# The fifth choice behind the fourth naming, other slots at which gather buffers join a ring, and the first query panel loaded into an area of its own

## The reference

```
u = expert_u[it]
h = jax.nn.gelu(jnp.einsum('td,tkd->tk', xt, u), approximate=False)
v = expert_v[it]
return jnp.einsum('tk,tkd->td', gt * h, v)
```

## Time and profile before

| | us |
|---|---|
| median of 3 runs (1876.32 to 1880.17) | 1878.65 |
| the profiled execution | 1875.81 |
| its span | 1874.0 |
| TensorE busy (matmul) | 1616.2 (86%) |
| VectorE busy | 997.8 (53%) |
| ScalarE busy | 454.4 (24%) |
| GpSimd busy | 314.4 (17%) |
| DMA, mean of the span | 252 GB/s |

### The profile page before, as it was taken

How to read it: one execution, slowest core, us unless ns; L and a number is a source line. 1 busy time by engine, 2 the same in 40 slices (tenths; PEclk the granted TensorE clock), 3 DMA queues, 4 the chain that set the end, 5 groups by cost and what they waited for, 6 DMA issues and landing times.

```text
span 1874.0 us, 19456 instructions
## 1 busy us (share of the span) xinstructions
PE 1616.2 (86%) x7688; PEld 1082.2 (58%) x7688; DVE 997.8 (53%) x1846; ACT 454.4 (24%) x1010; POOL 314.4 (17%) x269
## 2 busy tenths in 40 slices
PE   7999989999897887698938666677999999899998
PEld 6857656764755444245614222226998476479963
DVE  2433334331785775437997766663565414346654
ACT  1142142230333443213323322221000012310001
POOL 0000000000103533323426645520000000000000
PEclk9999989999998989899979988988999999999999
DMA  6444221126886999899999999993544443254443
GB/s 238 173 145 176 85 90 46 58 89 228 330 362 265 395 421 422 348 426 421 419 386 410 422 422 422 421 422 152 209 157 152 158 169 136 78 203 180 155 160 112
DMA packets 55192, 471.32 MB, mean 252 GB/s; under 512 B 6592, under 2 KB 7744, under 8 KB 10432
## 3 DMA queue, kind: packets, MB, share of 16 engines
q0 software_dynamic: 36864, 268.45, 34.6%
q1 hardware_dynamic: 18240, 201.66, 28.5%
HBM read 469.04 MB, written 1.05 MB: 251 GB/s over the span
## 4 chain that ended last, share of the span: by engine, by line
PE 63%; DMA 18%; DVE 10%; ACT 3%; issue 3%; POOL 2%; SPq 0%; DVEq 0%; ACTq 0%; POOLq 0%
PE ps L2381 13%; DMA main<-in_expert_uv,main 11%; PE ps L486 7%; PE ps L442 6%; PE ps L2538 5%; DMA panels<-in_expert_uv,main 5%; PE ps L412 5%; PE ps L1004 4%; PE ps L1242 4%; PE ps L2304 3%; PE ps L2308 3%; PE ps L482 3%; DVE main L938 2%; PE ps L2327 2%; DMA panels<-in_wall 2%
## 5 line engine op out<-in xcount | busy, mean ns | idle before, releaser
L1004 PE MATMUL ps<-main 128*128 128x512 f32 x636 | 320.6, 653 | 79.6 <-ACT main L985 72.8
L920 POOL DMA_INDIRECT main<-in_expert_uv,main x200 | 240.6, 1203 | 353.8 <-PE ps L1004 183.0
L938 DVE SCALAR_TENSOR_TENSOR main<-main 128x1024 f32<-128x1024 f32 x200 | 240.9, 1223 | 101.9 <-DMA main<-in_expert_uv,main 100.7
L1004 PEld LDWEIGHTS ps<-main 128*128 128x128 f32 x636 | 127.8, 210 | 252.5 <-issue 142.1
L1004 PE MATMUL ps<-panels,main 128*128 128x512 f32 x180 | 93.0, 660 | 53.5 <-ACT main L985 46.8
L973 ACT ACTIVATE main<-main 128x2 f32<-128x2 f32 x128 | 25.9, 203 | 399.7 <-DVE main L938 296.6
L442 PE MATMUL ps<-panels,xT 128*128 128x512 f32 x256 | 112.5, 592 | 0.0
L2381 PE MATMUL ps<-main 128*128 128x128 f32 x912 | 104.9, 275 | 0.0
L2381 PEld LDWEIGHTS ps<-main 128*128 128x128 f32 x912 | 103.4, 192 | 0.0
L1004 PEld LDWEIGHTS ps<-panels,main 128*128 128x128 f32 x180 | 36.1, 210 | 105.8 <-issue 70.3
L938 DVE SCALAR_TENSOR_TENSOR panels<-panels,main 128x1024 f32<-128x1024 f32 x56 | 67.5, 1223 | 43.4 <-DMA panels<-in_expert_uv,main 42.9
(11 more groups left out here) (318 smaller groups left out, 2395.0 us busy)
## 6 DMA issues: line engine op xcount, KB each, us to landing
panels<-in_wall SPq DMA_DIRECT2D x88, 2048.0 KB
main<-in_rows SPq DMA_DIRECT2D x14, 512.0 KB, 9.0
main<-in_expert_uv,main POOLq DMA_INDIRECT x200, 20.3
main<-in_sub_keys SPq DMA_DIRECT2D x2, 1024.0 KB, 13.3
mats<-in_mats SPq DMA_DIRECT2D x1, 1088.0 KB, 5.9
x<-in_x SPq DMA_DIRECT2D x2, 512.0 KB, 4.0
main<-in_pool_w SPq DMA_DIRECT2D x1, 1024.0 KB, 33.3
main<-in_rel_bias SPq DMA_DIRECT2D x1, 1024.0 KB, 15.2
```

The lines of the kernel that those rows point to most:

```text
L920: pool.indirect_dma_start(out=self.bufs[self.buf_of[r]], out_offset=None, in_=self.c.dram["expert_uv"], in_offset=bass.IndirectOffsetOnAxi ...
L938: dve.scalar_tensor_tensor(out=u, in0=u, scalar=1.0, in1=self.c.row(m, H2), op0=ALU.mult, op1=ALU.mult, accum_out=self.dots_at[:, m, q:q + ...
L1004: mm = pe.matmul(self.c.ps[:, b, :], self.diags[self.of_pe(r) % DIAG_RING], v[:, half * HALF:(half + 1) * HALF], start=(q == 1), stop=(q = ...
```

## The change

Four constants change: PANELS_FROM 12 to 15, PARTS_FROM 76 to 84, CHOICE_FREE 40 to 28, and QK_FIRST = 28 is new. In the order, top4, best4 and name4 of tile 0 stand between name3 and the two rows that follow it, and all hgrn1 pieces come after those, with two rows behind each. (So there are 73 rows before hgrn1's state instead of 70, and each later piece up to the cap at 128 comes three rows later.)

By the new spans row 12 gets the buffer of row 4, rows 13 and 14 those of rows 8 and 9, rows 15 to 18 the panel buffers; from 19 to 27 nine buffers go round, rows 28 to 30 get buffers 4 to 6, twelve go round to 59, eight from 60 to 83, and ten from 86. The row at CHOICE_FREE in tile 1 is now 156 instead of 168.

The ring of panels no longer holds qk's first panel: PLAN counts three for qk and WALL_AT skips one. SyncE loads the first into the 4096 floats from area 28 on, right behind the down panel that it issues at q = 3 of `stream`, with a semaphore of its own. The products with it are written out in `attention_tensor`, and use the two banks of the other parity; `keep_qk` reads them there. The loop of `stream` for down0 is no longer rolled, as its panels aren't consecutive in the wall.

```diff
-PLAN += WEIGHTS[[x for x, _ in WEIGHTS].index("ff0"):]
+PLAN += [(x, n - (x == "qk")) for x, n in WEIGHTS[[x for x, _ in WEIGHTS].index("ff0"):]]
...
-WALL_AT = [IN_WALL[x.split(".")[0]] + q for x, n in PLAN for q in range(n)]
+WALL_AT = [IN_WALL[x.split(".")[0]] + q + (x == "qk") for x, n in PLAN for q in range(n)]
...
-    def stream(self, sp, name, less=0):
+    def stream(self, sp, name, less=0, ahead=None):
...
             sp.wait_ge(self.panel_done.sem, first + q - 1)
             sp.dma_start(self.panels[:, slot, :], wall[at[q]]).then_inc(self.panel_loaded[slot].sem, 16)
+            if ahead == q:
+                sp.dma_start(self.area(D * QK_FIRST, PANEL), wall[IN_WALL["qk"]]).then_inc(self.first_qk_loaded.sem, 16)
...
-PANELS_FROM = 12
+PANELS_FROM = 15
 PANELS_UNTIL = 56
-PARTS_FROM = 76
-CHOICE_FREE = 40
+PARTS_FROM = 84
+CHOICE_FREE = 28
...
     part("beside1", 5)
     part("tile0", "name3")
     part("read1", 5)
+    part("tile0", "top4", "best4", "name4")
     rows(2)
     labels = ["k_t"] + [f"{x}{l}" for l in range(LEVELS) for x in ("span", "both", "a", "pick")]
-    for x in ("top4", "best4", "name4"):
-        part("hgrn1", labels.pop(0))
-        rows(1)
-        part("tile0", x)
-        part("hgrn1", labels.pop(0))
-        rows(2)
     for x in labels + ["ends"]:
         part("hgrn1", x)
         rows(2)
...
+        self.first_qk, self.first_banks = slot(QK_FIRST, KC, HALF), 2 * (1 - FIRST["qk"] % 2)
...
+        else:
+            pe.wait_ge(c.first_qk_loaded.sem, 16)
         pe.wait_ge(*c.at("xT_read", 2 + m))
-        products_by_tile(c, pe, "qk", (0,), m, True)
-    products_of_both(c, pe, "qk", (1,))
+        for j in range(2):
+            bank = t.first_banks + j
+            if m == 0:
+                pe.wait_ge(c.bank_read[bank].sem, c.bank_uses[bank])
+                c.bank_uses[bank] += 1
+            for half in range(2):
+                for k in range(KC):
+                    at = (2 * j + half) * P
+                    mm = pe.matmul(c.ps[:, bank, half * T + m * P:half * T + (m + 1) * P], t.first_qk[:, k, at:at + P],
+                                   c.xT[:, k, m * P:(m + 1) * P], start=(k == 0), stop=(k == KC - 1))
+            if m == 1:
+                mm.then_inc(c.up("first_qk"), 1)
+    products_of_both(c, pe, "qk", (0,))
...
-    c.stream(sp, "down0")
+    c.stream(sp, "down0", ahead=DOWN_SEVENS - 1)
```

More of the change, by code:

```diff
@@ L260, in __init__ @@
         self.hidden_made = sig("hidden_made")
+        self.first_qk_loaded = sig("first_qk_loaded")
         self.down_combined, self.h_combined = sig("down_combined"), sig("h_combined")
@@ L2689 @@
 ATTENTION_UNITS = ["s0.0", "s1.0", "s1.1", "s0.1", "s1.2", "s1.3", "a0.0", "a1.0", "a1.1", "o0", "o1", "t0", "t1"]
-QK_AT = (0, 2, 1, 3)
+QK_AT, QK_FIRST = (0, 2, 1, 3), 28
 GROUP_UNITS = [[("s0.0",), ("s1.0", "s1.1")], [("s0.1",), ("s1.2", "s1.3")]]
@@ L2762, in attention_tensor @@
     first_two = list(c.bank_uses)
-    products_of_both(c, pe, "qk", (2,), (0,))
+    products_of_both(c, pe, "qk", (1,), (0,))
     turned_back(first_two)
@@ L2766, in attention_tensor @@
     scores(1, 0)
-    products_of_both(c, pe, "qk", (2,), (1,))
+    products_of_both(c, pe, "qk", (1,), (1,))
     scores(1, 1)
-    products_of_both(c, pe, "qk", (3,))
+    products_of_both(c, pe, "qk", (2,))
     all_four = list(c.bank_uses)
@@ L2802, in keep_qk @@
     def keep_qk(q, j):
-        bank, at = wait_product(c, act, "qk", q, j), 4 * QK_AT[q] + 2 * j
+        at = 4 * QK_AT[q] + 2 * j
+        if q == 0:
+            bank = t.first_banks + j
+            act.wait_ge(*c.at("first_qk", 0, j + 1))
+        else:
+            bank = wait_product(c, act, "qk", q - 1, j)
         act.activation(t.qkT[:, at:at + 2, :], c.ps[:, bank, :].rearrange("p (k t) -> p k t", k=2),
```

## The result

The changed kernel takes 1860.85 us (median of 4 runs, 1859.38 to 1861.97) beside 1879.41 us of the kernel before on the same chip (1876.32 to 1884.14): ratio 0.9911, 95% interval 0.9891 to 0.9931, faster by 18.6 us. Measured again later, it took 1865.20 us (6 runs, 1861.74 to 1866.91): ratio 0.9920, interval 0.9900 to 0.9940. The forecast was 1860.7, in a range of 1854 to 1871. The two profiled executions differ by less than the medians: span 1874.0 before, 1860.2 after, 13.8 us.

A forecast was written before the change was run, and what follows sets the result against it. Full DMA engines were taken to bound the gather, so only their idle time could be won: gather 1.0 + 5.6 + 7.4 + 0 = 14.0, plus attention 4.0, 18.0 us; 1857.8, by the median 1860.7, range 1854 to 1871.

The forecast's parts named there:

- Choice 4, VectorE: Tile 0's fourth choice moved ahead of dots 11 and 12: its 16.1 us fill VectorE's 15.30 us gap.
- A: DMA idle at 552 to 573 us, 16.2 us: loses 2.5, gains 1.5, so 1.0 us won.
- B: DMA idle at 600 to 640 us: shrinks from 7.1 to about 1.5, 5.6 us won.
- rival 1: Gap at 600 to 640 us only moves, through later k_t and rows 19 and 20: won 12.4, 1866.3; chance 0.14.
- from slot 28 three more buffers help: Step for the 600 to 640 us gap: three more buffers join from slot 28, before from 40.
- C: DMA idle at 750 to 762 us, at the gate: recurrence buffers from 84 remove it, 7.4 us won.
- D: DMA idle at 970 to 985 us: keeps its 3.1 us, 0 won (bounds 4 lost to 3 won).
- what would show it: Signs listed, among them DMA share above 0.95 from 590 us and gathers ending about 14 us earlier.
- The 8 buffers: Rows 60 to 83 on 8 buffers instead of 12: price of less depth taken as 0.
- rival 4: Slower: 8 buffers don't keep the engines full over slots 60 to 83; 1884.9 at 3.5 us per row; chance 0.04.
- Attention: First query panel loaded aside: 2.5 us less wait and 1.6 us faster products, sum 4.0 us won.
- Rival 2: Tile 1 takes over, TensorE's path from the gate ruling: only 1.3, 3.5 and attention's 4.0 won, 1869.9; chance 0.12.

The follow-up runs named there:

- e4: Changed kernel with the two rows behind tile 0's fourth naming issued right behind the third, ahead of beside1 5 and read1 5; 1862.45 us, ratio 0.9912.
- e10: Changed kernel with CHOICE_FREE back at 40 instead of 28; 1863.33 us, ratio 0.9925.
- e8: Kernel before with the new order of the fourth choice and PARTS_FROM 79, other slots as before, no panel aside; 1876.21 us, ratio 0.9981.
- e7: Kernel before with the three new slot numbers (15, 84, 28), its own order and no panel aside; 1873.19 us, ratio 0.9964.
- e9: Kernel before with one constant changed, PARTS_FROM 84 instead of 76; 1874.94 us, ratio 0.9980.
- e2: Changed kernel with one row instead of two behind each of the first three hgrn1 pieces; 1863.94 us, ratio 0.9923.
- e3: Changed kernel letting rows up to 136 instead of 128 be issued beside tile 1's last two choices; 1859.74 us, ratio 0.9902.
- e12: Changed kernel with the edits of e2, e3 and e4 together; 1858.67 us, ratio 0.9898.

## Why the prediction was right, and where not

**The number.** 1860.7 against 1860.85, but this closeness is luck: the way shrank by 12.6 to 13.3 us where the sum said 18.0, and the first comparison stood some 5 us above that, most likely by chance. The gather, from row 11 to the last row, went from 701.0 to 693.0 us (692.0 in after again), 8.0 to 9.0 us where the sum said 14.0. The direction, the range and most of the steps stand on their own.

**Choice 4, VectorE.** Right. The 15.30 us gap is gone; choice 4 ends at 576.8 (forecast 576.5), dots 11 and 12 at 579.1 (578.8), and k_t runs at 587.47 (about 586) after 8.29 us of idle (about 7).

**A.** Row 12 at 550.38 (forecast 552), row 13 at 571.54 (572.6). Forecast 1.0 won; 0.1 to 1.1 is read. Right in substance: the early row fills what the burst, later against row 11, gives back (row 13 leaves 30.6 us behind row 11, before 30.2). e4 shows what A hangs on, the place of the sums before or behind a 7.3 us product.

**B, 5.6 forecast, 3.2 to 3.6 measured.** The hole at 600 to 640 closed, and a new one of 3.1 to 3.5 us opened ahead of it: row 19 left at 590.22, not 588, and row 20 at 592.09, not 590. That is rival 1 in small:
```profile
590.00:595.00 5.00, 5.00 (x24) 3.12 (x23) 3.27 (x6) 3.92 (x12) 3.56 (x2) 1.00 0.51 177
```
e10 shows that the step "from slot 28 three more buffers help" was wrong; the order alone closes B (e8: B is 0), and what is left of it in after comes with slot 15.

**C, 7.4 forecast.** Right, 7.5 measured, and by the means named: the slot number closes it (e7, e9). Wholly it does so only with the three rows more at the gate, which the working had as well. (Its "about 0.7 us later" should be 7.5 - 6.6 = 0.9; nothing hangs on it.) The gate's end came at 758.0, forecast 756.5; tile 1's first product at 777.28, forecast 777.

**D, the step that failed.** The sum had 0. D grew by 3.9 to 4.7 us. The working had VectorE's choices begin 10.8 us earlier and the add of row 128 come 14.3 us earlier, since three dots fewer stand among them. The choices began 13.2 us earlier (859.58 against 872.77), and 25 dots and not 28 stand among them, as forecast; but the add at 967.38 comes only 9.5 us earlier than that of before at 976.92. VectorE used the head start to wait: 10.1 us for rows that had not landed (the two above and two of 1 us), where before it waited 2.8. The rows came at 2.49 us each whatever VectorE did, and each choice piece now stood behind three later ones. I had taken the step's time for VectorE's work alone, and with it put the price of the later add at nothing. Relative to row 11, row 90 was issued 13.3 us earlier than before, row 142 only 8.3. e2 and e3 show the cause from both sides. In the part on what would show it, two signs failed for B and D: a share above 0.95 from 590 us on (0.51 from 590 to 595), and the gathers ending 14 us earlier (the last row was issued at 1233.92, before at 1243.15, 9.2 earlier).

**The 8 buffers.** Right for this kernel: 640 to 750 at share 1.01 and 421 GB/s, rival 4 falls. Its mechanism is real in small: with three rows fewer at the gate the 8 buffers lose 1.8 to 5.2 us (e9, e7, e12, e2). **Attention.** Right, 4.0 us in the trace, with gap 1.16 and products 7.38 as forecast; the granted clock from 1498 to 1506 was 1.00, where it had been 0.79. The Trainium skill (DMA: Bandwidth & Descriptors, Queues, rings and completion order) says that completion is not first in, first out for an issuing engine, which would allow the last down panel to finish late; it took 7.94 us, so this did not happen here.

**Rival 2, tile 1 takes over,** had the right place, tile 1's choices, but neither the mechanism nor the size: TensorE's path from the gate didn't rule (VectorE waited for rows), and it gave the gather 4.8 us in all, where 8.0 to 9.0 were won.

## What to carry over

Where a transfer engine paces a stretch, count what it stands idle and name the release that each hole hangs on; closing one hole opens the next when a piece that holds a release stands behind more rows than it did. A consumer that starts earlier gains nothing if its inputs come at a fixed rate: date a step by the later of its engine and its data. A busy share averaged over 100 us hides holes of 1 us; the amount moved in windows of 5 us shows them. And before a median difference of 5 us is explained, take the time between two events that enclose the change: here it agreed within 0.8 us in two traces of one kernel, where its medians of 4 and 6 runs moved by 4.

## What the runs showed of the hardware

The front of the kernel, same code in all of them, varies by up to 6.5 us to row 11's issue. Part of it is the granted clock: the same 16 products took 7.13 us in before, at a granted clock of 1.00 from 519 to 530 us, and 8.83 in after, at 0.84, where they had waited longer for their panel. TensorE's timelines, before and after:
```profile
521.15 7.13 PE L486 MATMUL ps<-panels,xT 128*128 128x512 f32 x16 [1.56 <-DMA panels<-in_wall]
```
```profile
519.78 8.83 PE L489 MATMUL ps<-panels,xT 128*128 128x512 f32 x16 [3.79 <-DMA panels<-in_wall]
```
The gather's full rate is steady: 421 to 424 GB/s between 770 and 860 us in eleven traces. The other three, e2, e7 and e12, have 418, 416 and 416 there at a share of 1.00 to 1.01. That is no slower engine: in e12 single windows of 5 us fall to 351 GB/s at share 0.94, and the windows at 715 and 765 us have 424.
